# The first normalisation and the first convolution columns run quarter by quarter of the features while their modulation weights load

## The chip, the cores and the metric

The kernel runs on one core of one Trainium2 chip. The metric is the device time in microseconds (us) of one launch, the median of several runs. PE is TensorE, with its weight loads listed apart as PEld; DVE is VectorE, ACT is ScalarE, POOL is GpSimd and SP is SyncE. "Clock" is the TensorE clock that was granted, as a share of 2.4 GHz: 0.50 is 1.2 GHz.

## The reference

Two sets of 128 tokens with 2048 features each, context tokens and latent tokens, go through two layers of a diffusion backbone. A conditioning vector makes six modulation vectors for each layer.

```
mod = silu(c) @ w_ada[l] + b_ada[l]          # 2048 x 12288: shift1, scale1, gate1, shift2, scale2, gate2
h   = rms_norm(x, g_attn) * (1 + scale1) + shift1
u_conv, q_g, k_g, v_g, q_w, k_w, v_w = split(h @ w_in[l])   # 2048 x 3584; the first 1024 columns are u_conv
a, gt = split(u_conv);  y = depthwise_conv31(a * sigmoid(gt)) ; layer norm; silu
... two attentions, both with grouped heads ...
x = x + gate1 * (concat(y_conv, y_g, y_w) @ w_out[l])
x = x + gate2 * (relu(h2 @ w_mlp1)**2 @ w_mlp2)     # h2: second modulated norm
```

After the two layers comes a last rms_norm. Everything is float32.

## The kernel before

**Tiles and products.** Features lie on partitions: `xT[128, 16, 256]` holds feature tile k for the 256 tokens. A large product splits both factors into a rounded part (`hi`, `hs[..., 0:256]`) and a rest (`lo`, `hs[..., 256:512]`) and sums three products: hi by both parts in one matmul of 512 columns, lo by the rounded part in one of 256. A weight matrix is used in pairs of 2 x 256 columns. Each pair is 8 slices of 512 rows by 256 columns: slice o is loaded by SP into `raw` (four slots of two slices, 1 MiB each, gated on `lo_ready`), copied by ACT into `hi` (`split_hi`, gated on `half_used` of three slices earlier), subtracted by DVE into `lo` (`split_lo`), and used by PE. The slots `hi` and `lo` hold four slices. The column pairs of `w_in` are seven, so its products have 56 steps of one slice. The first two pairs are the convolution's a and gate columns.

**Modulation vectors.** One vector is 16 units of `w_ada` of 128 rows by 2048 columns, 1 MiB each. The product of a unit is four matmuls, on four strips of 32 output partitions (`ada_products`). When the 16 units of a vector are summed, ACT copies the bank to `rows`, PE turns it (`ada_turn`) and DVE adds the bias (`add_bias`, counted in `mods_done`). Vectors 0 and 1 (shift1 and scale1) are loaded before anything else by POOL into eight slots (`pre_a`, `pre_q`, `ada`; `PRE_SLOTS`). A unit's slot is refilled when PE has used the unit eight before (`ada_used`). Later vectors use the two slots of `ada`, and their units are put behind certain steps of the products: `units_behind(step)` gives two units behind steps 2, 6, 10 and so on and a single one behind steps 36, 44, 48 and 52, 32 units in all.

**Order at the start.** PE: vector 0's units, transposes of the small parameters (`vrows`), `ada_turn(0)`, transposes of x, vector 1's units, `ada_turn(1)`, the sums of squares over features (`norm_sums`), `spread_rstd`, then step 0 of `w_in`. DVE makes the sums of squares in one reduction of `xsq`, and after vector 1 the normalised tiles of `hs`, 16 tiles one after another with ACT (`norm`). SP issues the small parameters, then x, and it holds the first `w_in` slots back with one wait:

```
sp.wait_ge(ada_used, 4 * PRE_JOBS - PRE_SLOTS - 1)     # 23 units used
```

**The 56 steps of `w_in` in one layer.** Each engine walks the same steps in `mixers(l)`, each followed by `mix_ops(l, step)`. DVE: step 9 and 17 `gate` (a times sigmoid of the gate columns, from `zc` in SBUF), then the 30 remaining taps of the convolution for two channel pairs, by `TAP_PLAN`: two taps of the first pair in steps 10 to 17, one in 18 to 31; one of the second pair in steps 18 to 45 (two in 33 and 34). A tap is two instructions of 128x256. From step 20 on come the squares, roots, rotations and scores of the heads. ACT copies half of each bank to `tmp` and DVE adds the other half, every four steps. The third vector's `ada_rows`, `ada_turn` and `add_bias` stand at steps 31, 32 and 33. The cached keys are turned at step 10.

Of the kernel before, what the change touches and what calls it, by code (L numbers as in the profile page):

```python
# [21 lines left out]
f32 = mybir.dt.float32  # L22
# [5 lines left out]
P = 128  # L28
S = 2
# [35 lines left out]
SINGLE_UNITS = (9, 11, 12, 13)  # L65

SHIFT1, SCALE1, GATE1, SHIFT2, SCALE2, GATE2 = (KT * n for n in range(6))

C_ID, C_PERM, C_COS, C_SIN, C_SEL = 0, 128, 256, 384, 512
CONSTS = 520  # L70
# [29 lines left out]
def build(nc, t):  # L100
# [45 lines left out]
    eps = place("eps", [P, 1], f32)  # L146
    warm = place("warm", [P, 1], f32)
    eps_sum = place("eps_sum", [P, 1], f32)
# [9 lines left out]
    xtok = place("xtok", [P, S, D], f32, hs_at)  # L158

# [21 lines left out]
    xsq = place("xsq", [P, KT, TOK], f32, hs_at + 16384)  # L181
# [5 lines left out]
    rstd_cols = pb[7][:, TOK:TOK + P], pb[6][:, 0:P]  # L187

# [4 lines left out]
    sel = cst[:, C_SEL:C_SEL + 8]  # L193

# [26 lines left out]
    x_turned, x_ready, xsq_ready, ssq_set = sem("x_turned"), sem("x_ready"), sem("xsq_ready"), sem("ssq_set")  # L221
# [45 lines left out]
    def units_behind(step):  # L267
# [9 lines left out]
        return []  # L277

# [20 lines left out]
    def vectors_done(layer, vector):  # L299

        return layer * VECTORS + vector // KT + 1
# [21 lines left out]
    def sums_left_out(layer, kind):  # L323


        return 2 * (2 * layer + (kind in ("up", "down")))
# [12 lines left out]
    with block:  # L339
# [3 lines left out]
        def _(sp):  # L343
            sp.dma_start(craw[:, 0, :], t["c_ctx"].rearrange("(p t) -> p t", t=KT)).then_inc(c_in, 16)
            sp.dma_start(craw[:, 1, :], t["c"].rearrange("a (p t) -> (a p) t", t=KT)).then_inc(c_in, 16)
            sp.dma_start(cst[:, :], t["consts"]).then_inc(consts_in, 16)
            sp.dma_start(sinks[:, :, :].rearrange("p l h -> p (l h)"),
# [15 lines left out]
            for s, name in enumerate(("x_prompt", "x_sample")):  # L363
                sp.dma_start(xtok[:, s, :], t[name].rearrange("a q d -> (a q) d")).then_inc(x_in, 16)
            sp.wait_ge(ada_used, 4 * PRE_JOBS - PRE_SLOTS - 1)

            for l in range(DEPTH):
# [5 lines left out]
                def load_mixers(l):  # L373
                    n = l * PAIRS_LAYER
                    for p in range(IN):
# [32 lines left out]
        def _(pool):  # L408
# [6 lines left out]
            src = t["w_ada"][0].rearrange("(p k) n -> p k n", k=KT)  # L415
            for u in range(4 * PRE_JOBS):
                after(pool, ada_used, u - PRE_SLOTS + 1)
                pool.dma_start(pre[u % PRE_SLOTS], src[:, u % KT, u // KT * D:(u // KT + 1) * D])\
                    .then_inc(pre_landed[u % PRE_SLOTS], 16)
# [7 lines left out]
        def _(pe):  # L427
            def norm_sums(l, c):


                final = (l, c) != (0, -2)
                if final:
                    pe.wait_ge(ssq_steps, ssq_base(l, c) + 1 + KT - 2)
                else:
                    pe.wait_ge(ssq_set, 1)
                for s in range(S):
                    mm = pe.matmul(pb[7][:, s:s + 1], ssq[:, s * P:(s + 1) * P], ones[:, 0:1],
                                   start=True, stop=not final)
                    for j in range(2 * final):
# [6 lines left out]
            def spread_rstd(q):  # L446
                pe.wait_ge(tok_rstd_ready, q + 1)
                for s in range(S):
                    pe.matmul(rstd_cols[s], tok_rstd[:, s:s + 1].to_broadcast([P, P]), ident,
                              start=True, stop=True).then_inc(rstd_spread, 1)  # L450
# [6 lines left out]
            def ada_unit(l, m, a, k):  # L457

                if k == 0:
                    pe.wait_ge(mods_done, l * VECTORS + m)  # L460
# [9 lines left out]
            def pre_vector(m):  # L470


                after(pe, mods_done, m)
                for k in range(KT):
                    u = KT * m + k
                    pe.wait_ge(pre_landed[u % PRE_SLOTS], 16 * (u // PRE_SLOTS) + 16)
                    ada_products(k, pre[u % PRE_SLOTS])

            def ada_turn(v):

                pe.wait_ge(rows_ready, v + 1)
# [8 lines left out]
            pre_vector(0)  # L490
            pe.wait_ge(vecs_in, 16 * 10 * DEPTH)
            for l in range(DEPTH):
                for b, r in ((0, P), (1, P), (2, MISC)):
                    mm = pe.transpose(pb[5 + 2 * l][:, b * P:b * P + r], vrows[0:r, l, b, :], ident[0:r, 0:r])
                mm.then_inc(vecs_turned, 1)
            ada_turn(0)
# [8 lines left out]
            pre_vector(1)  # L505
            ada_turn(1)

            for l in range(DEPTH):
# [63 lines left out]
                def mixers(l):  # L572
                    n = l * PAIRS_LAYER
                    for step in range(8 * IN):
                        p, g, h = step // 8, step // 4 % 2, step % 4
                        if h == 0:
# [7 lines left out]
                        for u in units_behind(step):  # L584
# [33 lines left out]
                def mix_ops(l, step):  # L618
# [3 lines left out]
                    if step == 10:  # L622
# [20 lines left out]
                    if step == 32:  # L643
# [106 lines left out]
                def stage(name, c, l=l):  # L750
                    if name in ("norm1", "norm2"):
                        norm_sums(*((l, -1) if name == "norm2" else (l - 1, CHUNKS - 1) if l else (0, -2)))
# [14 lines left out]
        def _(act):  # L767
            def split_hi(n, o):

                s, sub = chunk_place(n, o)  # L770
                act.wait_ge(raw_landed[s], 16 * (n + o // 8 + 1))
# [3 lines left out]
            def ada_rows(v):  # L775
                act.wait_ge(ada_used, KT * v + KT)
                after(act, modps_ready, v)
# [4 lines left out]
            ada_rows(0)  # L782
# [5 lines left out]
            for b in range(8):  # L788
                s, q = b % 2, b // 2
                act.wait_ge(x_turned, b + 1)  # L790
                act.activation(xT[:, 4 * q:4 * q + 4, s * P:(s + 1) * P],
                               pb[b % 4][:, :].rearrange("p (k q) -> p k q", k=4), ACT.Copy).then_inc(x_ready, 1)
            act.wait_ge(x_ready, 8)
            act.activation(xsq[:, :, :], xT[:, :, :], ACT.Square).then_inc(xsq_ready, 1)
            ada_rows(1)
            for o in range(3):
                act.wait_ge(raw_landed[o // 2], 16)
                act.activation(hi[:, o, :, :], raw[:, o // 2, 4 * (o % 2):4 * (o % 2) + 4, :], ACT.Copy)\
                   .then_inc(hi_ready, 1)

            for l in range(DEPTH):
# [63 lines left out]
                def mix_ops(l, step):  # L865
# [3 lines left out]
                    if step == 0:  # L869
# [4 lines left out]
                    if step in (8, 16):  # L874
# [3 lines left out]
                    if step == 11:  # L878
                        drain_turn(1, kcT[:, :, :], "p (v d) -> p v d", v=4)
                    if step == 20:  # L880
                        act.wait_ge(bank_freed, n4 + 10)
                        act.wait_ge(conv_tap, TAP_OPS * l + TAPS_DONE[17])
# [13 lines left out]
                    if step == 31:  # L896
# [107 lines left out]
                def norm(q, shift, l=l):  # L1004
                    act.wait_ge(stat_ready, q + 1)
# [3 lines left out]
                    for k in range(KT):  # L1009
                        for s in range(S):  # L1010
                            act.wait_ge(norm_y, q * NORM_STEPS + S * k + s + 1)
                            act.activation(hs[:, k, s * P:(s + 1) * P], ybuf[:, 2 * (k % UNROLL_K) + s, :], ACT.Identity,
                                           bias=mods[:, l, shift + k, s:s + 1]).then_inc(norm_hi, 1)

                def stage(name, c, l=l):
                    if name == "norm1":
# [6 lines left out]
            act.wait_ge(stat_ready, 2 * DEPTH + 1)  # L1023
# [12 lines left out]
        def _(dve):  # L1036
# [7 lines left out]
            def add_bias(l, m):  # L1044

                dve.wait_ge(modps_ready, l * VECTORS + m + 1)
# [14 lines left out]
            for s in range(S):  # L1061
                dve.tensor_tensor(cT[:, :, s:s + 1], craw[:, s, :].unsqueeze(2), csig[:, s, :].unsqueeze(2),
                                  ALU.mult).then_inc(c_ready, 1)
            dve.wait_ge(sinks_in, 16)
            own.done(dve.tensor_scalar(nsinks[:, :, :], sinks[:, :, :], -1.0, None, ALU.mult))
            dve.wait_ge(vecs_ready, 1)
            add_bias(0, 0)
            dve.wait_ge(xsq_ready, 1)
# [396 lines left out]
```

## Time and profile before

| | us |
|---|---|
| median of the runs (3 runs, 2327.01 to 2327.36) | 2327.07 |
| the profiled execution's own time | 2326.37 |
| its span, first to last instruction | 2324.7 |
| PE busy | 2254.8 (97%) |
| DVE busy | 1459.3 (63%) |
| ACT busy | 1096.3 (47%) |

The profiled execution is 0.7 us below the median, and 1.7 us of its time lie outside its span. All stretches below are in us from the start of the span. The opening is the stretch up to 122 us; steps 3 to 55 of the first layer's `w_in` follow it.

### The profile page before, as it was taken

How to read it: one execution, taken by the hardware profiler on the slowest of the kernel's cores; microseconds unless marked ns; L12 is line 12 of the kernel's file. 1: busy time of each engine (PE TensorE's matmuls, PEld its weight loads, DVE VectorE, ACT ScalarE, POOL GpSimd, SP SyncE). 2: the span in 40 equal slices, each digit the busy share in tenths (PEclk: the TensorE clock that was granted, in tenths of full speed). 3: DMA queues.
4: the chain of work that ended last, by engine and by line, in shares of the span. 5: the costliest groups of instructions: out<-in, count | busy, mean ns of one | idle time of the engine just before them, and what ended most of it. 6: DMA issues, size and time to landing. Idle time of an engine off the chain costs nothing.

```text
span 2324.7 us, 36272 instructions
## 1 busy us (share of the span) xinstructions
PE 2254.8 (97%) x13442; PEld 1831.4 (79%) x13442; DVE 1459.3 (63%) x2521; ACT 1096.3 (47%) x1739; POOL 101.9 (4%) x196
## 2 busy tenths in 40 slices
PE   5799999999999999999999999999999999999998
PEld 0378777778887887887787777887788888888887
DVE  0379655655655665565567876667566666666665
ACT  0344564544444444444445445645445444445444
POOL 2000000000000000000000000000000000000000
PEclk7699999999999999999999999999999999999999
DMA  9988868698589679768955877566956556655652
GB/s 384 366 317 290 292 232 323 230 334 283 192 278 316 209 223 327 250 193 299 315 182 194 328 286 264 197 197 228 317 175 186 183 184 201 192 181 185 195 188 102
DMA packets 390005, 570.66 MB, mean 245 GB/s; under 512 B 9540, under 2 KB 364408, under 8 KB 365048
## 3 DMA queue, kind: packets, MB, share of 16 engines
q1 hardware_dynamic: 359928, 365.51, 49.0%
q0 software_dynamic: 27648, 201.34, 21.9%
q10 hardware_dynamic: 2304, 2.10, 0.3%
q8 instruction: 85, 1.39, 0.2%
q14 instruction: 40, 0.33, 0.0%
HBM read 565.76 MB, written 3.15 MB: 245 GB/s over the span
## 4 chain that ended last, share of the span: by engine, by line
PE 90%; DVE 4%; DMA 4%; ACT 2%; issue 1%; POOL 0%; ACTq 0%; POOLq 0%
PE bank L530 44%; PE bank L533 21%; PE bank L607 9%; PE bank L466 6%; PE bank L610 4%; DMA ada<-in_w_ada 4%; DVE hs L1321 1%; DVE ybuf L1313 1%; PE bank L551 1%; PE bank L554 1%; ACT hi L773 0%; DVE lo L1041 0%; PE bank L730 0%; PE bank L483 0%; PE bank L707 0%
## 5 line engine op out<-in xcount | busy, mean ns | idle before, releaser
L1041 DVE TENSOR_TENSOR lo<-raw,hi 128x1024 fp32r<-128x1024 f32 x685 | 820.8, 1223 | 400.7 <-ACT hi L773 400.3
L773 ACT ACTIVATE hi<-raw 128x1024 fp32r<-128x1024 f32 x685 | 706.3, 1054 | 447.3 <-PE bank L533 314.8
L530 PE MATMUL bank<-act,hi 128*128 128x512 f32 x2304 | 724.7, 396 | 1.2 <-DVE tsum L1160 1.2
L530 PE MATMUL bank<-hs,hi 128*128 128x512 f32 x2048 | 652.2, 400 | 7.8 <-DVE hs L1321 4.5
L533 PEld LDWEIGHTS bank<-act,lo 128*128 128x128 f32 x2304 | 432.8, 188 | 102.4
L533 PEld LDWEIGHTS bank<-hs,lo 128*128 128x128 f32 x2048 | 386.7, 189 | 92.3
L533 PE MATMUL bank<-act,lo 128*128 128x256 f32 x2304 | 452.7, 278 | 0.0
L533 PE MATMUL bank<-hs,lo 128*128 128x256 f32 x2048 | 404.3, 279 | 0.0
L530 PEld LDWEIGHTS bank<-act,hi 128*128 128x128 f32 x2304 | 350.7, 189 | 5.6 <-issue 4.2
L530 PEld LDWEIGHTS bank<-hs,hi 128*128 128x128 f32 x2048 | 313.4, 190 | 43.7 <-issue 37.2
L607 PE MATMUL bank<-hs,hi 128*128 128x512 f32 x896 | 292.9, 408 | 7.9 <-DVE hs L1321 4.6
L826 ACT ACTIVATE tmp<-bank 128x256 f32<-128x256 f32 x336 | 110.7, 382 | 395.9 <-PE bank L533 318.1
L1095 DVE TENSOR_TENSOR tsum<-bank,tmp 128x256 f32<-128x256 f32 x272 | 114.5, 421 | 207.6 <-ACT tmp L826 207.6
L610 PEld LDWEIGHTS bank<-hs,lo 128*128 128x128 f32 x896 | 170.3, 190 | 40.6
L610 PE MATMUL bank<-hs,lo 128*128 128x256 f32 x896 | 178.1, 280 | 0.0
L466 PE MATMUL bank<-ada,cT 128*32 128x512 f32 x1344 | 168.4, 615 | 8.6 <-DMA ada<-in_w_ada 8.6
L607 PEld LDWEIGHTS bank<-hs,hi 128*128 128x128 f32 x896 | 139.3, 191 | 23.0 <-issue 13.7
L413 POOL DMA_DIRECT2D ada<-in_w_ada x160 | 84.7, 529 | 1510.2 <-PE bank L466 1482.7
L832 ACT ACTIVATE thid<-xT 128x256 f32 (+1 forms) x160 | 66.9, 418 | 163.0 <-DVE xT L1127 153.4
L1127 DVE SCALAR_TENSOR_TENSOR xT<-tsum,mods,xT 128x128 f32 (+1 forms) x304 | 93.5, 349 | 36.2 <-DVE tsum L1095 34.9
L1238 DVE SCALAR_TENSOR_TENSOR yconv<-hpad,vecs,yconv 128x256 f32<-128x256 f32 x240 | 100.9, 477 | 0.0
L466 PEld LDWEIGHTS bank<-ada,cT 128*32 128x32 f32 x1344 | 34.3, 110 | 76.4 <-issue 42.9
(151 smaller groups left out, 1174.1 us busy)
## 6 DMA issues: line engine op xcount, KB each, us to landing
raw<-in_w_mlp SPq DMA_DIRECT2D x256, 1024.0 KB, 5.9
ada<-in_w_ada POOLq DMA_DIRECT2D x168, 1024.0 KB, 7.6
raw<-in_w_in SPq DMA_DIRECT2D x56, 1024.0 KB, 5.3
raw<-in_w_out SPq DMA_DIRECT2D x32, 1024.0 KB, 5.6
pre_a<-in_w_ada POOLq DMA_DIRECT2D x16, 1024.0 KB, 17.0
pre_q<-in_w_ada POOLq DMA_DIRECT2D x8, 1024.0 KB, 17.8
xtok<-in_x_prompt SPq DMA_DIRECT2D x1, 1024.0 KB, 14.2
xtok<-in_x_sample SPq DMA_DIRECT2D x1, 1024.0 KB, 32.5
```

The lines of the kernel that those rows point to most:

```text
L413: pool.dma_start(ada[:, k % 2, :], src[:, k, bass.ds(m * D, D)]).then_inc(ada_landed[k % 2], 16)
L466: mm = pe.matmul(ada_ps[32 * q:32 * q + 32, :], cT[:, k, :], unit[:, q * 512:(q + 1) * 512], start=(k == 0), stop=(k == KT - 1))
L530: pe.matmul(pb[2 * g + j][:, :], hi[:, h, k, j * P:(j + 1) * P], acts[:, k_, :], start=(k_ == 0), stop=False)
L533: mm = pe.matmul(pb[2 * g + j][:, TOK:2 * TOK], lo[:, h, k, j * P:(j + 1) * P], acts[:, k_, 0:TOK], start=False, stop=(k_ == KT - 1))
L607: pe.matmul(pb[2 * g + j][:, :], hi[:, slot, k, j * P:(j + 1) * P], acts[:, 4 * x + k, :], start=start, stop=False)
L610: mm = pe.matmul(pb[2 * g + j][:, TOK:2 * TOK], lo[:, slot, k, j * P:(j + 1) * P], acts[:, 4 * x + k, 0:TOK], start=False, stop=stop)
L773: act.activation(hi[:, o % 4, :, :], raw[:, s, 4 * sub:4 * sub + 4, :], ACT.Copy).then_inc(hi_ready, 1)
L826: act.activation(tmp[:, j, :], pb[2 * g + j][:, TOK:2 * TOK], ACT.Copy).then_inc(tmp_ready, 1)
L1041: dve.tensor_tensor(lo[:, o % 4, :, :], raw[:, s, 4 * sub:4 * sub + 4, :], hi[:, o % 4, :, :].bitcast(f32), ALU.subtract).then_inc(lo_read ...
L1095: dve.tensor_tensor(tsum[:, j, :], bank, tmp[:, j, :], ALU.add).then_inc(bank_freed, 1)
L1127: dve.scalar_tensor_tensor(x, total[:, :, s * P:(s + 1) * P], mods[:, l, bass.ds(gate + 4 * i + 2 * g + j, 1), s], x, ALU.mult, ALU.add).t ...
L1238: dve.scalar_tensor_tensor(y, hpad[:, ch, :, tap:tap + P], vecs[:, l, 1, 4 * tap + ch:4 * tap + ch + 1], y, ALU.mult, ALU.add).then_inc(co ...
```

## The change

- A unit of the first two vectors is now a quarter q of both: 2 x 128 rows by 512 columns of vector 0 and 512 columns of vector 1, in two transfers of POOL. Eight units make one quarter. There are still 32 units, 1 MiB each, in eight slots.
- x is loaded ahead of the small parameters on SP's queue and turned first on PE. DVE, no longer ACT, copies its banks. ACT squares `xtok` with a running sum over features (`accum_out`), so PE's `norm_sums` and DVE's reduction fall away for the first norm.
- When quarter q is summed, its four feature tiles of shift1 and scale1 are made (`quarter_turn`, one `rows` copy, a bias add), DVE and ACT normalise tiles 4q to 4q+3, and PE runs four slices on them (`open_chunk`): the same four k tiles for all four column groups of the two convolution pairs. The four groups stay open in banks 0 to 3 over all quarters. Between the slices stand the next quarter's units.
- An open slice adds both halves of `hs` into one 256-column range: six matmuls of 256 columns for each k and j pair, not two of 512 and two of 256. No `tmp` copy and no add follow. ACT takes the sigmoid and DVE the product `a * sigmoid(gt)` straight from PSUM (`open_gate`).
- SP loads the 16 open slices in 8 slots, each in two transfers, gated one by one on `ada_used` (`RAW_GATES`).
- Steps 0 to 15 of the first layer no longer exist in `mixers`. Two units of vector 2 stand behind slice 13, the other 30 behind steps 18 to 54 (`UNITS_FIRST`: alternately 2 and 1 on even steps). The first layer's taps are one of each pair in every step 16 to 45. The rows, turn and bias add of vector 2 stand at steps 35, 35 and 36; the cached keys are turned at step 18.

```diff
+RAW_GATES = (5, 6, 12, 14, 20, 22, 28, 30)
 @@ sync
+            for s, name in enumerate(("x_prompt", "x_sample")):      # now ahead of sinks and vrows
+                sp.dma_start(xtok[:, s, :], ...).then_inc(x_in, 16)
-            sp.wait_ge(ada_used, 4 * PRE_JOBS - PRE_SLOTS - 1)
+            for j in range(OPEN_STEPS // 2):
+                after(sp, lo_ready, 2 * j - 6)
+                sp.wait_ge(ada_used, RAW_GATES[j])
+                for g in range(2):
+                    sp.dma_start(raw[:, j % 4, 4 * g:4 * g + 4, :], w_conv[:, j // 2, g, :, j % 2, :])...
 @@ gpsimd
-                pool.dma_start(pre[u % PRE_SLOTS], src[:, u % KT, u // KT * D:(u // KT + 1) * D])...
+                for m in range(2):
+                    pool.dma_start(unit[:, :, m, :], src[:, 2 * kk:2 * kk + 2, m, 512 * q:512 * q + 512])...
 @@ tensor
+            for u in range(8):
+                quarter_unit(u)
+            pe.wait_ge(vecs_ready, DEPTH)
+            spread_rstd(0)
+            quarter_turn(0)
+            for q in range(QUARTERS - 1):
+                for o in range(4 * q, 4 * q + 3):
+                    open_chunk(o)
+                    for u in (0, 1) if o % 4 < 2 else (0, 1, 2, 3):
+                        quarter_unit(8 * (q + 1) + 2 * (o % 4) + u)
+                quarter_turn(q + 1)
+                open_chunk(4 * q + 3)
+            for o in range(12, 16):
+                open_chunk(o)
+                if o == 13:
+                    for u in range(OPEN_UNITS):
+                        ada_unit(0, 2, PRE_JOBS, u)
 @@ scalar
+            for q in range(QUARTERS):
+                act.wait_ge(ada_used, 8 * q + 8)
+                after(act, modps_ready, q)
+                act.activation(rows[:, :], ada_ps[:, :], ACT.Copy).then_inc(rows_ready, 1)
+                act.wait_ge(mods_done, q + 1)
+                norm_tiles(0, SHIFT1, 0, range(4 * q, 4 * q + 4))
+                for o in range(4 * q + (2 if q else 0), 4 * q + 6):
+                    split_hi(0, o, o < OPEN_STEPS)
+                    if o == 16:
+                        open_sigmoid(0)
+            split_hi(0, 18)
+            open_sigmoid(2)
 @@ vector: the same loop with the bias add, gains(), norm_tiles(), split_lo() and open_gate()
-                    for step in range(8 * (IN + 1)):
+                    for step in range(OPEN_STEPS if l == 0 else 0, 8 * (IN + 1)):
```

## Rows read from the trace of the kernel before

**Rows 1.** Busy time by stretch: start:end, length, engines, granted clock, DMA share, GB/s

```profile
22.00:54.00 32.00, 19.08 (x88) 2.04 (x88) 0.00 (x0) 0.00 (x0) 5.28 (x10) 0.55 1.01 418
64.00:68.00 4.00, 4.00 (x42) 1.24 (x44) 0.00 (x0) 3.97 (x3) 1.58 (x3) 1.00 1.01 426
75.00:97.00 22.00, 14.31 (x64) 1.57 (x64) 0.82 (x1) 0.03 (x1) 0.86 (x2) 0.58 1.03 414
107.00:110.00 3.00, 3.00 (x10) 2.52 (x10) 3.00 (x13) 1.95 (x7) 0.00 (x0) 0.50 0.82 290
...
165.20:222.10 56.90, 56.90 (x353) 44.73 (x352) 51.47 (x101) 24.99 (x34) 4.22 (x8) 1.00 0.81 294
222.10:281.80 59.70, 59.70 (x395) 47.82 (x393) 41.90 (x91) 31.79 (x66) 4.22 (x8) 1.00 0.81 299
```

**Rows 2.** The chain that ended last, from 74 us to step 3

```profile
74.81 20.11 DMA ada<-in_w_ada
...
94.97 1.98 PE bank L466 x8
96.97 0.61 ACT rows L778
...
97.62 1.89 PE bank L483 x8
...
119.55 1.57 DVE hs L1321 x6
```

**Rows 3.** DMA in 0:95, then 24:70, 75:90 and 95:98: packets, MB, share

```profile
DMA packets 7779, 37.86 MB, mean 399 GB/s; under 512 B 1172, under 2 KB 3297, under 8 KB 3425
q0 software_dynamic: 4608, 33.56, 85.7%
...
DMA packets 2919, 19.42 MB, mean 422 GB/s; under 512 B 356, under 2 KB 562, under 8 KB 562
...
q0 software_dynamic: 764, 5.55, 87.6%
q1 hardware_dynamic: 763, 0.78, 14.6%
...
DMA packets 1151, 1.16 MB, mean 387 GB/s; under 512 B 16, under 2 KB 1151, under 8 KB 1151
```

**Rows 4.** The timeline: start, length, engine, line, instructions merged

```profile
9.10 7.96 SPq L362 DMA_DIRECT2D vrows<-in_conv_b  x1
...
26.98 0.53 POOL L418 DMA_DIRECT2D ada<-in_w_ada  x1 [2.31 <-PE bank L466]
...
104.19 1.81 DVE L1313 SCALAR_TENSOR_TENSOR ybuf<-xT,amul,bank 128x128 f32<-128x128 f32 x6 [0.89 <-PE bank L449]
...
106.68 1.19 PE L607 MATMUL bank<-hs,hi 128*128 128x512 f32 x2 [2.09 <-DVE hs L1321]
...
108.09 1.05 PE L607 MATMUL bank<-hs,hi 128*128 128x512 f32 x2
...
109.38 1.05 PE L607 MATMUL bank<-hs,hi 128*128 128x512 f32 x2
...
148.73 0.66 PE L691 MATMUL bank<-cst,ktokc 128*128 128x128 f32 x4
...
160.46 1.92 PE L466 MATMUL bank<-ada,cT 128*32 128x512 f32 x16
...
165.20 0.63 PE L607 MATMUL bank<-hs,hi 128*128 128x512 f32 x2
...
167.99 0.63 PE L607 MATMUL bank<-hs,hi 128*128 128x512 f32 x2
...
430.97 0.64 PE L551 MATMUL bank<-act,hi 128*128 128x256 f32 x4
...
431.69 0.64 PE L551 MATMUL bank<-act,hi 128*128 128x256 f32 x4
```

**Rows 5.** DVE and ACT in the steps of `w_in`

```profile
147.04 1.06 ACT L773 ACTIVATE hi<-raw 128x1024 fp32r<-128x1024 f32 x1 [1.72 <-PE bank L610]
...
159.29 1.21 DVE L1041 TENSOR_TENSOR lo<-raw,hi 128x1024 fp32r<-128x1024 f32 x1
160.43 1.66 DVE L1238 SCALAR_TENSOR_TENSOR yconv<-hpad,vecs,yconv 128x256 f32<-128x256 f32 x4
```

**Rows 6.** Issue to landing of `ada`, us min/median/max, 120 to 330 us

```profile
DMA to landing us min/median/max: 4.9/6.8/10.5
```

More of the change, by code:

```diff
@@ L265, in mixer_vector, with units_behind @@
         return layer * VECTORS + (2 if layer == 0 else 3)
-    def units_behind(step):
+    def units_behind(l, step):
+        if l == 0:
+            return [FIRST_UNIT[step] + u for u in range(UNITS_FIRST.get(step, 0))]
         half = step // 4
@@ L299, in vectors_done @@
     def vectors_done(layer, vector):
-        return layer * VECTORS + vector // KT + 1
+        return event(layer * VECTORS + vector // KT + 1)
     def q_rstd(h):
@@ L1008, in norm @@
                     act.wait_ge(mods_done, vectors_done(l, shift))
[L1009 to L1013, printed above, removed]
+                    norm_tiles(q, shift, l, range(KT))
                 def stage(name, c, l=l):
-                    if name == "norm1":
+                    if name == "norm1" and l:
                         norm(2 * l, SHIFT1)
@@ new lines, in first_tap, with clear_halo @@
+            def first_tap(l, first):
+                for ch in (first, first + 1):
+                    dve.tensor_scalar(yconv[:, ch, :].rearrange("p (s q) -> p s q", s=S),
+                                      hpad[:, ch, :, 0:P], vecs[:, l, 1, ch:ch + 1],
+                                      vecs[:, l, 1, V_CONVB + ch:V_CONVB + ch + 1], ALU.mult, ALU.add)\
+                       .then_inc(conv_tap, 1)
+            def clear_halo():
+                own.done(dve.memset(hpad[:, :, :, 0:HALO].rearrange("p c s q -> p (c s) q"), 0.0))
+                own.done(dve.memset(hpad[:, :, :, HALO + P:2 * HALO + P].rearrange("p c s q -> p (c s) q"), 0.0))
@@ new lines, in gate @@
+            def gate(l, first, a):
+                own.wait(own.n)
+                dve.wait_ge(gate_sig, 2 * l + first // 2 + 1)
+                dve.tensor_tensor(
+                    hpad[:, first:first + 2, :, HALO:HALO + P].rearrange("p c s q -> p (c s) q"), a,
+                    zc[:, CT + first:CT + first + 2, :].rearrange("p c (s q) -> p (c s) q", s=S), ALU.mult)\
+                   .then_inc(conv_gated, 1)
+                dve.wait_ge(conv_gated, 2 * l + first // 2 + 1)
+                first_tap(l, first)
@@ L1139, in mixers @@
                     n = l * PAIRS_LAYER
-                    for step in range(8 * (IN + 1)):
+                    for step in range(OPEN_STEPS if l == 0 else 0, 8 * (IN + 1)):
                         p, g = step // 8, step // 4 % 2
@@ L1395, in tap_plan @@
                     count[tap, ch] = n
-        done[step] = n
     assert n == TAP_OPS and next(a, None) is None and next(b, None) is None
-    return plan, count, done
+    return plan, count
 HEAD_GROUPS = (0, 1, 2, 3, 4, 5, 6, 8, 10)
-TAP_PLAN, TAP_COUNT, TAPS_DONE = tap_plan()
+TAP_PLAN, TAP_COUNT = zip(*(tap_plan(layer) for layer in range(DEPTH)))
 ROPES = ((26, KG), (28, QG), (30, QG + 2), (34, QG + 4), (42, KW), (46, WIN_Q[0]), (49, WIN_Q[2]), (53, WIN_Q[4]))
```

331 lines of the change are left out of this document (195 added, 136 removed).

## The prediction, made before the changed kernel was run

> **What bounds the kernel now.** I read the page first: PE is busy 97% of the span, so the whole is bound by TensorE, and the only stretch where a change can win much is one in which PE has no work or works slowly. The busy time by stretch finds it. From 22 to 54 us PE is busy 19.1 of 32 us at a granted clock of 0.55, from 75 to 97 us 14.3 of 22 us at 0.58, and in both the DMA share is 1.0 at 418 and 414 GB/s [rows 1]. The reader is to see there that the opening is bound by the transfer of `w_ada`, and that PE's low figure is a queue that waits for it. The chain that ended last says the same: it runs through a landing of `ada` for 20.1 us up to the last unit at 94.97, then through `rows`, the turn, and DVE's 16 tiles up to 121 us [rows 2]. After that nothing but PE counts: from 165.2 to 281.8 us it is busy for all 116.6 us at full clock [rows 1].
>
> So the opening costs 122 us in which PE does three slices of `w_in` and the vectors' products. The change puts 16 slices in there. PE work that it takes out of the time behind is worth its full length; what it adds to the transfer costs its full length as well, since DMA is the bound.
>
> **Reference point.** Step 16 starts at 165.20 and step 17 at 167.99, so a slice is 2.79 us at full clock [rows 4]. I work out when step 16 starts in the new kernel.
>
> **The transfer of the opening.** By 95 us 37.86 MB have moved, of which 33.56 MB are the 32 units [rows 3]; x (2.10 MB) and the small parameters (about 0.4 MB) are in the rest, which leaves 1.8 MB of `raw`. In the new order the last unit is preceded by seven of the eight open `raw` slots (7.34 MB), since the eighth is gated on 30 used units. That is 33.56 + 2.1 + 0.4 + 7.34 = 43.4 MB, 5.5 MB more, and at 415 GB/s 13.4 us. The runs of a unit shrink from 8 KB to 2 KB. No row shows 2 KB: 8 KB runs went at 422 GB/s and 1 KB runs alone at 387 [rows 3]. The ends are 0 and 7.2 us for 33.56 MB; I take 410, nearer to the large runs since a queue of many runs kept its rate at 1 KB within 8%, so 2.3 us. The last unit then lands at 94.9 + 13.4 + 2.3 = 110.6 us. Each unit is also two transfers now. The trace shows 32 units in 95 us, 2.9 us each with eight outstanding, so no fixed time for each transfer is visible when others are queued behind it, and I add none.
>
> The Trainium skill, "DMA: Bandwidth & Descriptors", section "Anatomy of one DMA", gives a fixed 2.0 us for each transfer plus its bytes at 436 GB/s and, in "Bandwidth", advises at least 1 MiB for each transfer, which speaks against cutting the units in two. Taken one after another, 64 transfers would be an estimated 205 us, and already the 32 of before would be 141 us, where the trace has 95; so the trace disagrees for a full queue, and the sum goes by the trace.
>
> **What may keep the queue from being full.** (a) The start. x lies ahead of the small parameters now. Before, q0's and q1's packets alternated one for one from 75 to 90 us (764 and 763) although one was eight times as long [rows 3], so with 2 KB units x's long runs get the larger share, and the SP stall of 7.96 us at a small parameter [rows 4], which I read as its short runs waiting one by one behind 8 KB runs, should shrink. I place x at 10 to 14 us and the first unit's use at 22 to 28 us, before the eight slots are full at about (8.4 + 2.5) / 0.42 + 3 = 29 us. No bubble. If x landed only at 30 us, PE would start at 39 and DMA would idle 10 us; this end stays in the range. (b) PE's order. ACT splits slices 4 and 5 before it copies `rows` of quarter 1. Their slot is gated on 12 used units, needs some 7 us to land (the median of `ada` under such load is 6.8 [rows 6]) and 2.1 us to split [rows 5], while PE needs about 6.6 us (a slice and four units). PE stands for a few us, and the same again in quarters 2 and 3. The eight slots ahead hold 20 us of transfer, which covers most of it. I add 2.5 us (0 to 8). Last unit landed: 113.1.
>
> (c) POOL issues 512 runs for a unit instead of 128. A unit's issue took 0.53 us [rows 4]; the ends are 1.1 us (by transfer) and 2.1 us (by run), both under the 2.5 us that a unit's bytes take. Nothing.
>
> **PE in the opening.** One quarter at full clock: four slices at 0.72 us for each k (430.97 to 431.69, the same six-matmul form), 2.88 each and 11.5 together; eight units at 0.93 (1.85 for two), 7.4; turn and wait for `rows` 1.6. Sum 20.5 us. At 1.2 GHz a k takes 1.29 (108.09 to 109.38), a unit 1.98 and the turn 1.89: 38 us [rows 2, 4]. DMA needs (8.39 + 2.1) / 0.415 = 25.3 us for a quarter. Warm, PE is hidden with 5 us to spare; cold, it is the bound. With 20.5 of 25.3 us busy, in dense pieces, I expect mostly full clock: the dense stretch from 64 to 68 us had 1.00, the ones with 60% and 65% busy 0.55 and 0.58 [rows 1].
>
> The Trainium skill, "TensorE: Matmul & The Clock Gate", Part 1, says that the array starts throttled and that sustained activity releases it; the rows at 64 and at 75 us agree in direction. It would leave the sum as it is.
>
> DVE in a quarter: 4.2 us of tiles (1.04 each) and four `lo` of 1.21, 9 of 25 us; ACT less. Both are hidden, as are the x copies, the squares and the removed reduction.
>
> **Behind the last unit.** 113.1 + product 1.98 + `rows` 0.61 + turn 1.89 (half clock, since PE waited for transfers [rows 2]) = 117.6. Slice 11 at the half clock's 1.29 for each k: 5.1, to 122.7. DVE's first tile is ready 0.4 + 2.5 us after the turn (104.19 to 106.68 [rows 4]), 120.5, so slice 11 covers it. Slices 12 to 15: 11.5, and two units 1.85. Step 16 starts at 136.1 instead of 165.2: 29.1 us earlier.
>
> **What is owed later.** Before step 16 the old kernel had done eight units of vector 2, the new one two: 6 x 0.93 = 5.6 us. The turn of the cached keys moves behind: 0.6 us. The first layer's other 40 steps are the same products. The bias add of vector 2 now stands at DVE's step 36, and PE's unit behind step 36 waits for it: behind the start of step 36 come `hi` 1.06, `lo` 1.21, four taps 1.66 and the add 0.19, 4.1 us [rows 5], against 2.8 us of products. 1.5 us (0 to 3).
>
> **Steps 16 to 45.** DVE had 93.4 us of work in 116.6 us [rows 1]; 24 more tap instructions at 0.42 minus a gate of 1.4 make 102, and PE gets five more units, 121. Not the bound in the sum; within a step it is 1.21 + 1.66 against 2.79 and more. DMA: 30 slices (15 MiB) and 21 units are 37.7 MB in 121 us, 312 GB/s, below 415. Nothing.
>
> **Sum.** 29.1 - 5.6 - 0.6 - 1.5 = 21.4 us. Against the profiled execution: 2326.4 - 21.4 = 2305.0; its median stood 0.7 us higher, so 2305.7 us.
>
> **Rivals.**
> 1. *All orders hidden, PE warm to the end.* No 2.5 us, no 1.5 us, slice 11, the turn and the unit at full clock (2.2 + 0.9 + 1.0): 29.5 us gained, 2297.6. For it speaks the backlog of eight slots; against it that PE waits for single units at the end, as from 75 to 97 us.
> 2. *PE becomes the bound of the opening by its clock.* If half of a quarter's work runs at 1.2 GHz, it takes 29.3 us, 4.0 more than DMA, three times: 12 us, 2318. Waits for `raw` between slices would keep it so. At 1.2 GHz throughout, 12.7 x 3 = 38 us are lost: 2344, slower than before. It ends slower from 68% of the work at 1.2 GHz on.
> 3. *A unit's two transfers of 2 KB runs take longer than its bytes*, in POOL's issue or in the queue. From 4.2 us for a unit on (134.5 / 32) the change loses; at 5 us the last unit lands at 160: 2353. Rows for 1 KB runs at 387 GB/s and 0.53 us of issue speak against it.
> 4. *Later steps wait.* `ada` has two slots; a unit needs 6.8 us from issue (median), and behind steps 18 to 36 the next one is due after two slices and a unit, 5.6 to 6.6 us. Up to 1.2 us at nine places is 11 us: 2317. Before, the same density stood only in steps 44 to 54, which are longer.
> 5. *The gain is eaten whole*, by 10 us of idle transfer at the start and rival 2 in part: 2326.
>
> **How the numbers follow.** Forecast 0.42, with a range of its own from 2300 to 2311; rival 1 0.17; rival 2 0.15 in part and 0.03 as slower; rival 3 0.04; rival 4 0.15; rival 5 0.04. A change of 0.2% (4.7 us) is about what the measurement tells from none. Slower is rival 2's end, rival 3 and a share of 5: 0.08; same 0.05, faster 0.87. The range reaches from a little below rival 1 (2294, with 422 GB/s kept) to just past 2 and 4 (2320), and leaves out 3, 5 and 2's end.
>
> **What would show it.** The last product of a quarter unit should start near 113 us and step 16 near 136; DMA share 1.0 from 3 to 110 us, at 410 GB/s or more; clock above 0.8 from 45 to 100 us; PE busy all the way from step 16 with a gap of 1 to 3 us at step 36 only. A last unit past 125 us shows rival 2, 3 or the bubble: by the clock, by POOL's instructions, or by a DMA share below 1 near 30 us. Waits of PE for `ada` behind steps 20 to 36 show rival 4.

## The result and the profile after

| | before | after |
|---|---|---|
| median of the runs, us | 2327.04 (4 runs, 2326.48 to 2327.36) | 2344.68 (4 runs, 2343.03 to 2346.91) |
| the profiled execution and its span, us | 2326.37, 2324.7 | 2343.03, 2341.3 |
| last unit of vectors 0 and 1 used, us | 96.9 | 151.8 |
| step 16 starts, us | 165.2 | 170.8 |
| second norm of layer 0 (`spread_rstd`), us | 447.2 | 463.4 |

The ratio is 1.0077, 95% interval 1.0059 to 1.0094: slower by 17.6 us, where 21.4 us less was forecast. By the two profiled executions step 16 comes 5.6 us later, and from there to the second norm it takes 292.6 us instead of 282.0, 10.6 more. What follows adds 0.4. That makes the 16.6 us between the spans.

Busy time by stretch of the changed kernel, with the columns of [rows 1]:

```profile
3.00:151.00 148.00, 82.16 (x582) 57.12 (x586) 33.54 (x78) 28.56 (x49) 44.58 (x62) 0.78 0.78 295
...
30.00:40.00 10.00, 6.90 (x38) 2.29 (x42) 0.00 (x0) 0.81 (x2) 2.66 (x4) 0.58 0.30 106
50.00:60.00 10.00, 0.00 (x0) 0.00 (x0) 0.93 (x2) 1.78 (x2) 0.00 (x0) 0.50 1.04 411
66.00:70.00 4.00, 4.00 (x35) 2.56 (x35) 2.36 (x2) 2.00 (x2) 2.66 (x4) 1.00 0.27 81
80.00:90.00 10.00, 0.00 (x0) 0.00 (x0) 0.00 (x0) 0.00 (x0) 2.92 (x5) 0.64 1.04 410
96.00:100.00 4.00, 4.00 (x21) 4.00 (x21) 4.00 (x14) 3.02 (x8) 0.00 (x0) 0.51 0.09 30
100.00:110.00 10.00, 10.00 (x83) 6.86 (x83) 1.69 (x2) 1.06 (x1) 3.78 (x6) 1.00 0.44 128
120.00:130.00 10.00, 0.67 (x4) 0.67 (x4) 2.12 (x2) 2.49 (x3) 0.22 (x1) 0.52 1.04 411
140.00:150.00 10.00, 10.00 (x88) 6.94 (x88) 0.00 (x0) 0.00 (x0) 0.00 (x0) 1.00 0.32 105
...
170.77:463.40 292.63, 288.18 (x1858) 223.98 (x1856) 196.69 (x382) 142.67 (x253) 24.32 (x46) 1.00 0.85 306
```

Before, the transfer was full throughout the opening and PE filled in behind it. Here the two take turns. From 50 to 60, from 80 to 90 and nearly all of 120 to 130 us PE does nothing while the transfer is full. From 66 to 70, from 100 to 110 and from 140 to 150 PE is busy all the time at full clock while the transfer runs at 0.27, 0.44 and 0.32. Over 148 us it moves 295 GB/s, 43.7 MB: the amount that was forecast (43.4), not the rate (410 and more).

The chain of waits says what PE stands for (start, length, what):

```profile
18.80 14.25 DMA vrows<-in_g_final
...
41.62 16.58 DMA raw<-in_w_in
...
73.25 16.94 DMA raw<-in_w_in
...
91.17 1.04 ACT hi L843
...
92.75 1.87 PE bank L512 x8
...
110.15 16.62 DMA raw<-in_w_in
...
148.20 2.76 PE bank L503 x24
```

Where [rows 2] had landings of `ada`, here stand three landings of an open slot of `raw`, each some 16.7 us (from the issue of its second half), and one of the small parameters. PE's waits from 10 to 350 us (what, total us, times, longest):

```profile
PE bank L512 <- ACT rows L880: 27.3, 3, 13.3
PE bank L527 <- DVE lo L1126: 15.1, 1, 15.1
PE bank L556 <- DMA vrows<-in_g_final: 13.7, 1, 13.7
PE bank L550 <- DMA xtok<-in_x_sample: 13.5, 1, 13.5
PE bank L491 <- DMA ada<-in_w_ada: 1.6, 3, 0.9
PE bank L491 <- DVE mods L1133: 1.0, 1, 1.0
```

The first line is the one to read with care. PE waits for ACT's copy of `rows`, which takes 0.6 us; ACT stands before it at `split_hi` of slices 4q+4 and 4q+5, and those wait for `raw`. The timeline has the step:

```profile
90.21 2.00 ACT L843 ACTIVATE hi<-raw 128x1024 fp32r<-128x1024 f32 x2 [21.82 <-DMA raw<-in_w_in]
92.12 0.58 ACT L880 ACTIVATE rows<-bank 128x512 f32<-128x512 f32 x1
```

And the packets, from 73.2 to 90.2 us, while the chain waits for its second slot; q0 is POOL's queue of units, q1 is SP's queue of `raw`:

```profile
DMA packets 2846, 6.80 MB, mean 400 GB/s; under 512 B 198, under 2 KB 1521, under 8 KB 2845
...
q0 software_dynamic: 1490, 5.42, 80.4%
q1 hardware_dynamic: 1355, 1.35, 22.9%
```

As in [rows 3] the two queues get about one packet each in turn. A packet of q0 is now 3.6 KB (5.42 MB / 1490), one of q1 is 1 KB, so `raw` gets a fifth of the bytes, 79 GB/s. Within one burst of work PE has released the units' slots, and POOL has filled its queue with the next units. The Trainium skill, "DMA: Bandwidth & Descriptors", section "Queues, rings and completion order", says that a DMA engine goes round its queues packet by packet; the counts agree. A `raw` slot is 1024 packets, and by equal counts they come with 1024 packets of units: 1024 x 4.6 KB at 400 GB/s is an estimated 12 us. The page has 16.6 as the median of the 16 transfers, two for each slot:

```profile
raw<-in_w_in SPq DMA_DIRECT2D x16, 512.0 KB, 16.6
```

The packets say where the rest goes. The slot's first half is issued at 72.84, and up to 75.0 us q1 moves nothing. By 86.4 it has moved 1015 packets, so the slot's 1024 are through near 86.5:

```profile
q1 hardware_dynamic: 1015, 1.02, 22.2%
```

It counts as landed only at 90.2 us, when some 300 packets more than its own (1355 less 1024) have moved on q1, for the next slot. So of the 17.4 us from the first issue some 3 pass ahead of the first packet, 11 in the sharing and 3.7 behind. The other two slots have about 3, 12 and 2. Why a slot starts 3 us after its issue and counts as landed so late isn't shown.

Then comes the other half of the turn-taking. By 96 us the units have landed as well, and POOL's next issue is at 104.18, since PE first does the turn and two slices and frees no slot before that:

```profile
104.18 2.88 POOL L447 DMA_DIRECT2D pre_a<-in_w_ada  x4 [21.26 <-PE bank L503]
```

### The profile page after: what moved, and what is told of

It reads as the page before. It is cut to its first block, busy times and chain, and to the rows that moved or that the text cites. A ratio compares the mean times of both kernels' runs of the same rounds, so it can differ in the third digit from the quotient of the medians.

```text
span 2341.3 us, 36628 instructions
## 1 busy us (share of the span) xinstructions
PE 2242.5 (96%) x13582; PEld 1844.6 (79%) x13582; DVE 1455.8 (62%) x2525; ACT 1090.4 (47%) x1728; POOL 131.0 (6%) x228
## 4 chain that ended last, share of the span: by engine, by line
PE 88%; DMA 4%; DVE 4%; ACT 2%; SPq 1%; issue 1%; ACTq 0%; POOLq 0%; POOL 0%; DVEq 0%
PE bank L598 43%; PE bank L601 21%; PE bank L677 7%; PE bank L491 6%; PE bank L680 3%; DMA raw<-in_w_in 2%; DMA ada<-in_w_ada 2%; PE bank L619 1%; PE bank L527 1%; DVE hs L1182 1%; DVE ybuf L1174 1%; PE bank L503 1%; ACT hi L843 1%; PE bank L622 1%; DMA vrows<-in_g_final 1%
## 5 line engine op out<-in xcount | busy, mean ns | idle before, releaser
L598 PE MATMUL bank<-hs,hi 128*128 128x512 f32 x2048 | 652.4, 400 | 7.7 <-DVE hs L1182 4.4
L601 PEld LDWEIGHTS bank<-hs,lo 128*128 128x128 f32 x2048 | 386.8, 189 | 92.3
L601 PE MATMUL bank<-hs,lo 128*128 128x256 f32 x2048 | 404.4, 279 | 0.0
L598 PEld LDWEIGHTS bank<-hs,hi 128*128 128x128 f32 x2048 | 313.6, 190 | 43.5 <-issue 36.8
L677 PE MATMUL bank<-hs,hi 128*128 128x512 f32 x768 | 250.7, 408 | 3.7 <-DVE hs L1182 2.1
L680 PEld LDWEIGHTS bank<-hs,lo 128*128 128x128 f32 x768 | 145.4, 189 | 34.4
L491 PE MATMUL bank<-ada,cT 128*32 128x512 f32 x1280 | 155.9, 599 | 2.8 <-DMA ada<-in_w_ada 1.8
L680 PE MATMUL bank<-hs,lo 128*128 128x256 f32 x768 | 152.3, 280 | 0.0
L677 PEld LDWEIGHTS bank<-hs,hi 128*128 128x128 f32 x768 | 119.4, 191 | 17.3 <-issue 12.3
L907 ACT ACTIVATE act<-thid 128x256 fp32r<-128x256 f32 x128 | 53.5, 418 | 67.2 <-DVE thid L1254 67.2
## 6 DMA issues: line engine op xcount, KB each, us to landing
raw<-in_w_in SPq DMA_DIRECT2D x16, 512.0 KB, 16.6
```

The lines of the kernel that those rows point to most:

```text
L491: mm = pe.matmul(ada_ps[32 * q:32 * q + 32, :], cT[:, k, :], unit[:, q * 512:(q + 1) * 512], start=(k == 0), stop=(k == KT - 1))
L598: pe.matmul(pb[2 * g + j][:, :], hi[:, h, k, j * P:(j + 1) * P], acts[:, k_, :], start=(k_ == 0), stop=False)
L601: mm = pe.matmul(pb[2 * g + j][:, TOK:2 * TOK], lo[:, h, k, j * P:(j + 1) * P], acts[:, k_, 0:TOK], start=False, stop=(k_ == KT - 1))
L677: pe.matmul(pb[2 * g + j][:, :], hi[:, slot, k, j * P:(j + 1) * P], acts[:, 4 * x + k, :], start=start, stop=False)
L680: mm = pe.matmul(pb[2 * g + j][:, TOK:2 * TOK], lo[:, slot, k, j * P:(j + 1) * P], acts[:, 4 * x + k, 0:TOK], start=False, stop=stop)
```

## The experiments

Each was compared with the kernel before on its own chip (medians there 2327.48, 2327.52 and 2327.74 us). The ratio is to the kernel before; that of the changed kernel is 1.0077. "Step 16" is its start in the profiled execution.

| | median (range, runs) | ratio, 95% | step 16 |
|---|---|---|---|
| e1 | 2313.47 (2311.17 to 2317.93, 4) | 0.9944, 0.9928 to 0.9961 | 139.6 |
| e2 | 2331.48 (2328.11 to 2334.60, 10) | 1.0015, 1.0005 to 1.0024 | 157.3 |
| e3 | 2337.22 (2335.45 to 2339.12, 4) | 1.0046, 1.0029 to 1.0063 | 162.7 |
| e4 | 2331.76 (2330.62 to 2334.05, 10) | 1.0020, 1.0010 to 1.0030 | not the same opening |
| e5 | 2331.71 (2330.51 to 2336.64, 9) | 1.0019, 1.0009 to 1.0029 | 158.5 |
| e6 | 2308.23 (2306.92 to 2308.31, 4) | 0.9917, 0.9901 to 0.9934 | 135.3 |
| e7 | 2314.18 (2309.76 to 2319.23, 4) | 0.9950, 0.9933 to 0.9967 | 136.3 |
| e8 | 2315.14 (2313.64 to 2316.70, 4) | 0.9949, 0.9933 to 0.9966 | 134.0 |
| e9 | 2313.05 (2308.53 to 2313.52, 5) | 0.9932, 0.9919 to 0.9946 | 139.2 |

**e1: the open `raw` slots are issued early.** The first four slots are issued with no gate, the others eight used units sooner, and the gate of 30 used units stands behind them.

```diff
-RAW_GATES = (5, 6, 12, 14, 20, 22, 28, 30)
+RAW_GATES = (0, 0, 0, 0, 12, 14, 20, 22)
-                sp.wait_ge(ada_used, RAW_GATES[j])
+                after(sp, ada_used, RAW_GATES[j])
+            sp.wait_ge(ada_used, 30)
```

> The changed kernel, but each open raw slot is asked for about eight used units earlier: the first four as soon as SP is through the small parameters, the others at 12, 14, 20 and 22 used units; the pairs behind still wait for 30. Theory A (the slots are asked for too late; a slot takes 16.6 us to land beside POOL's backlog, PE stands for it three times, 42 us in all, and the transfers then stand for want of free units): the three waits go, the last unit is used near 118 us instead of 151, step 16 starts near 140 instead of 171, and the time is 2307 to 2318 us. Theory B (the waits come from the order of ACT's and DVE's work; the landing is not what is late): the waits stay within a few us, 2335 to 2345. Theory C (the transfers as such are slower in the new form): DMA share 1.0 throughout but the last unit past 135 us.

31.2 us less than the changed kernel in the median, and step 16 31.2 us earlier. PE's waits and the busy time by stretch:

```profile
PE bank L528 <- DVE lo L1127: 6.0, 1, 6.0
...
PE bank L513 <- ACT rows L881: 2.2, 3, 0.7
```

```profile
3.00:116.00 113.00, 75.75 (x578) 49.92 (x578) 35.69 (x80) 29.81 (x50) 45.14 (x63) 0.91 1.03 403
```

The wait for `rows` falls from 27.3 to 2.2 us, which is three copies; the one for `lo` from 15.1 to 6.0. The transfer is full to the last unit. A slot still takes 15.1 us to land, median of the page: the landing hasn't become shorter, it lies where nobody waits for it. The mean clock in the opening rises from 0.78 to 0.91 with no edit to PE, so the low clock was a sequel of the waits. The result is theory A's.

**e2: the small parameters are turned after the first quarter's units.** Only PE's order is changed.

```diff
+            for u in range(8):
+                quarter_unit(u)
             pe.wait_ge(vecs_in, 16 * 10 * DEPTH)
             ... transposes of vrows ...
-            for u in range(8):
-                quarter_unit(u)
```

> The changed kernel, but PE uses the first eight units before it waits for the small parameters and turns them. PE stood 14 us for them, and the transfers stood from about 31 to 37 us. Theory A (idle transfer in the opening is lost for good): the first unit is used near 20 us, as soon as it has landed and the turns of x are done, the transfers do not stop near 30 us, and 5 to 10 us are gained: 2335 to 2340 us. Rival (the slots of raw set the pace, so what is gained at the start is lost again in the first wait for raw): within 2 us of 2344.7.

13.2 us less than the changed kernel: the wait for `vrows` was worth its length. The first unit is used at 18.9 us instead of 34.8, and the wait for `rows` stays at 26.9 us. It is more than either theory had (5 to 10 us, or within 2).

**e3: each quarter splits its own slices only.** ACT and DVE copy `rows` and add the bias of the next quarter before they split that quarter's slices.

```diff
-                for o in range(4 * q + (2 if q else 0), 4 * q + 6):
+                for o in range(4 * q, 4 * q + (6 if q == 3 else 4)):
```

> The changed kernel, but ACT and DVE split slices 4q and 4q+1 in their own quarter, behind its normalised tiles, so that the copy of rows for the next quarter no longer stands behind slices whose raw slot is late. Theory A (the landing itself is late): the waits move from the turn to the first slice of each quarter, PE gets one slice and a turn ahead but pays for the split behind the tiles; 2338 to 2345 us. Theory B (the order was the fault): the waits of 13 us at the turns vanish and are not found elsewhere; 2315 to 2325.

7.5 us less. The wait changes its name and mostly stays:

```profile
PE bank L527 <- DVE lo L1126: 33.7, 4, 15.2
...
PE bank L512 <- ACT rows L880: 2.2, 3, 0.7
```

The three landings on the chain are 16.6, 16.0 and 16.6 us. The waits at `rows` and `lo` are 35.9 us instead of 42.4. So ACT's order costs some 7 us of them, and the rest is the landing, which is only seen at another place. Theory A's mechanism holds, with a little more gained than it had.

**e4: the kernel before, each of its 32 units cut into two transfers of 2 KB runs** (abridged).

```diff
-                pool.dma_start(pre[u % PRE_SLOTS], src[:, u % KT, ...])...
+                for m in range(2):
+                    pool.dma_start(unit "p (b m n)"[:, :, m, :], src "p (b m n)"[:, :, m, :])...
```

> The kernel before, but every one of its first 32 units is loaded in two transfers of 512 KB with runs of 2 KB, to the same places. Measures the disputed price of the new form of the transfers by itself. Theory A: 2 to 7 us of lower rate (410 to 390 GB/s instead of 422 over 33.6 MB), the opening's last unit at 97 to 102 us instead of 95: 2329 to 2334 us. Theory C (a fixed 2 us for each transfer, or a slow issue by POOL): 20 us and more, 2347 us or above. With no price at all: 2327.

4.3 us more than the kernel before in the median, and the last unit's product starts at 100.03 instead of 94.97 us. Packets from 0 to 100 us, and by queue from 70 to 100:

```profile
DMA packets 13583, 39.08 MB, mean 391 GB/s; under 512 B 1701, under 2 KB 5004, under 8 KB 13324
...
q0 software_dynamic: 2599, 9.44, 77.2%
q1 hardware_dynamic: 2772, 2.80, 26.3%
```

By 100 us 39.08 MB have moved, 1.2 MB more than by 95 us before [rows 3], and q0's part of both is the 32 units' 33.56 MB. The 1.2 MB are `raw`, which got ahead by one packet for each, now smaller, packet of a unit: 3 of the 5 us. The other 2 are the rate, 391 GB/s against 399. Thirty-two more transfers for 4.3 us are 0.13 us each. The rule of the Trainium skill that the prediction weighed, a fixed 2.0 us for each transfer ("DMA: Bandwidth & Descriptors", section "Anatomy of one DMA"), would have had 64 us for them; it doesn't show while others are queued.

**e5: half of each open slot is issued on ACT's queue.** The gates are those of the changed kernel.

```diff
-                for g in range(2):
-                    sp.dma_start(raw[:, j % 4, 4 * g:4 * g + 4, :], ...)
+                sp.dma_start(raw[:, j % 4, 0:4, :], ...)            # SP: first half
+            def open_half(j):                                       # ACT: second half
+                act.wait_ge(ada_used, RAW_GATES[j])
+                act.dma_start(raw[:, j % 4, 4:8, :], ...)
```

> The changed kernel, but the second half of each open raw slot is issued by ACT on its own queue, under the same gates; SP issues the first half. In the changed kernel the queue of raw got one packet for each of POOL's (705 and 709 from 82 to 90 us), 1 KB against 3.6 KB, so a slot landed 16.6 us after its issue. Theory A1 (the share of the queue sets the landing): two queues get two packets for one of POOL's, a slot lands in 8 to 10 us, the three waits of PE shrink by 6 to 8 us each, and the time is 2320 to 2330 us. Theory A2 (a slot lands only when the units queued ahead of it are through): the landing stays at 15 to 17 us, and the time within 3 us of 2344.7.

13.0 us less than the changed kernel. From 40 to 56 us three queues share, and the chain has shorter landings:

```profile
q0 software_dynamic: 1290, 4.68, 77.3%
q1 hardware_dynamic: 720, 0.72, 12.8%
q10 hardware_dynamic: 714, 0.71, 12.7%
```

```profile
41.57 12.79 DMA raw<-in_w_in
...
68.12 12.89 DMA raw<-in_w_in
...
100.51 12.53 DMA raw<-in_w_in
```

With the same bytes, gates and backlog a slot lands 3.8 to 4.1 us sooner, three times, and PE's waits for `rows` and for the first slice fall from 42.4 to 29.5 us. Equal counts on three queues would have 512 packets of each beside the slot's halves, 512 x 5.6 KB at 400 GB/s, an estimated 7 us instead of 12. So a second queue takes off about a quarter of the landing, nearly what the counts give. That is less than theory A1 had (8 to 10 us for a landing, 2320 to 2330), since by the packets of the changed kernel some 5 us of a landing lie ahead of and behind the sharing; A2 is out.

**e6: e1 and e2 together.**

> Both edits at once: the raw slots asked for early, and the first eight units used before the small parameters. Theory (the transfer is now the only bound of the opening; the early run's DMA share is already 1.0 from 20 to 120 us): the earlier start of PE brings nothing more or 1 to 3 us, last unit used at 112 to 116 us, 2309 to 2314 us. Rival (the 14 us wait of PE at the start is on the path): another 8 to 13 us, 2300 to 2305.

36.5 us less than the changed kernel, 19.3 less than the kernel before: the fastest of all. It is less than the sum of e1 and e2, 44.4 us, and lies between the theory (2309 to 2314) and the rival (2300 to 2305): the transfer is now full from 3 to 113 us, and from 100 to 116 us PE is busy without a gap too, so little is left to gain from either alone:

```profile
3.00:113.00 110.00, 79.90 (x558) 54.55 (x559) 33.53 (x78) 27.57 (x48) 44.70 (x62) 0.84 1.03 403
100.00:116.00 16.00, 16.00 (x136) 10.63 (x137) 4.73 (x7) 4.01 (x4) 0.00 (x0) 1.00 0.90 349
```

```profile
114.71 1.90 PE L504 MATMUL bank<-ada,cT 128*32 128x512 f32 x16
117.33 1.06 PE L513 MATMUL bank<-cst,rows 128*128 128x4 f32 x8 [0.72 <-ACT rows L881]
```

The last turn ends at 118.4 us, where the prediction's sum had 117.6, and step 16 starts at 135.3, where it had 136.1.

**e7: e6, e3's order, and the last two slots late** (gates 22 and 28), to keep the bytes of the last slices behind the last units.

> As the run with both edits, and ACT and DVE split slices 4q and 4q+1 in their own quarter, with the last two open slots gated at 22 and 28 used units. Theory (bytes ahead of the last unit set its landing; with the split in its own quarter a late slot no longer blocks the rows): up to 1 MiB less ahead of the last unit, 2 us earlier, but 2 to 3 us more behind the last quarter's tiles: 2309 to 2315 us, the same as without.

Not faster than e6, and within the forecast. The wait for `rows` falls to 2.1 us, and the one for `lo` rises to 14.8 us at four places; step 16 is 1.0 us later. In the median it is 5.9 us slower than e6, with a wide range (2309.76 to 2319.23); its profile, at the lower end of it, shows 2.5 us by the second norm.

**e8: e6 with one unit of vector 2 behind each of the steps 18 to 31 and 34 to 49**, its `rows` and turn at step 32 and its bias add at 33.

```diff
-UNITS_FIRST = {18: 2, 20: 1, 22: 2, 24: 1, 26: 2, ...}
-VECTOR_STEP = (34, 31)
+UNITS_FIRST = {step: 1 for step in (*range(18, 32), *range(34, 50))}
+VECTOR_STEP = (31, 31)
```

> As the run with both edits, but the 30 later units stand one behind each of steps 18 to 31 and 34 to 49, and vector 2's rows, turn and bias at steps 32, 32 and 33. In the changed kernel PE waited 1 us for the bias add at step 36 and 2 to 4 us for landings of ada. Theory (pairs of units in two slots leave 6.6 us for a landing of 7.2): the bias wait goes and the ada waits mostly: 2 to 4 us less than the run with both edits. Rival (these waits cost nothing at the end, since the heads' steps behind are set by other work): within 1 us of it.

6.9 us slower than e6, all of it behind step 16: 299.7 us to the second norm against 292.1. PE waits for `ada` at five places and for ACT's `esink`, a wait of 0.4 us in the changed kernel:

```profile
PE bank L491 <- DMA ada<-in_w_ada: 3.3, 5, 1.0
...
PE bank L788 <- ACT esink L1080: 3.1, 3, 1.4
```

The wait for the bias add is gone, but what took its place costs more: 3.7 us of idle time and 3.9 of busy time over e6. A unit that stands alone takes PE 1.06 us, two together 1.85 (e6); the 46 units up to the second norm take 47.4 us here and 45.3 in the changed kernel. Neither the theory (2 to 4 us less) nor the rival (within 1 us) held: even spacing is not what the later steps lack.

**e9: e6 with slices 0 and 1 split ahead of the first `rows`**, and gates (0, 0, 0, 0, 8, 8, 16, 16).

> As the run with both edits (raw slots early, small parameters late; 2308.2 us), and slices 0 and 1 are split ahead of the first rows copy and the first bias add, and the later four open slots are asked for at 8, 8, 16 and 16 used units instead of 12, 14, 20 and 22. In the run with both edits PE still stood 6.0 us for the first slice's lo and 6.3 us for rows behind late slots, and from 100 to 120 us it was busy without a gap while the DMA share fell to 0.79, so PE sets the end of the opening there. Theory (these two waits are what is left before PE): 5 to 8 us less PE time ahead of the last unit, which the transfer (43.4 MB at 0.41 MB/us, 109 us) allows to about 110 instead of 115.7: 2302 to 2305 us. Rival (the transfer already sets it): within 1.5 us of 2308.2.

Not faster than e6: 4.8 us slower in the median, but the fastest of its runs, 2308.53, is near e6's, and the two intervals of the ratio overlap. Both the theory (2302 to 2305) and the rival (within 1.5 us of e6) miss. In the profiled one step 16 is 3.9 us later. ACT, and with it the first `rows`, now waits for a slot (6.4 us of the 8.6 that PE waits for `rows`). More `raw` ahead of the last units may also put these back; that is not shown by itself. The chain, with the turn at half clock again:

```profile
95.28 20.59 DMA ada<-in_w_ada
...
118.56 1.87 PE bank L513 x8
```

## Why the prediction was wrong

**The step that failed** is (b) of "what may keep the queue from being full", PE's order. It saw the mechanism: `rows` of the next quarter stands behind the split of slices 4 and 5, whose slot is issued with some 6.6 us of PE work left. It then put the slot's landing at "some 7 us", from the median of `ada` [rows 6], and let "the eight slots ahead" cover most of the rest: 2.5 us in all (0 to 8). Both parts were wrong. The landing is 16.6 us and more. [Rows 6] are from the steps of `w_in`, where two units are outstanding; in the opening POOL has up to eight queued, and the prediction itself had the row for that, a landing of `ada` of 20.11 us on the chain [rows 2]. The kernel before even has the same stream in the same place: its first two slots of `raw`, issued from 71.4 us on beside the last units, land after 24.8 us in the median:

```profile
raw<-in_w_in SPq DMA_DIRECT2D x2, 1024.0 KB, 24.8
```

And the backlog that was to cover the wait is what makes the slot slow: PE works off eight units in one go, POOL queues eight new ones, the `raw` slot issued in the middle has to share with them. When PE goes on they have landed or nearly so, and PE has a turn and slices to do before it frees their slots again. In this time the transfer has little or nothing: 0.27 from 66 to 70, 0.09 from 96 to 100, 0.44 and 0.32 in the windows. The waits are 27.3 us at `rows` and 15.1 us at the first slice, 42.4 in all; e1, which only issues these slots sooner, gives back 31.2.

**The start, (a).** x landed as placed (PE waits for it 13.5 us), the queue was not: the small parameters held PE until 33.1 us, and the first unit was used at 34.8, outside the "22 to 28". The prediction took the 7.96 us stall at a small parameter as the thing that shrinks (it is 5.71 us now) and did not add up their landing, 14.25 us on the chain, behind which PE's program puts the first unit. The transfer was empty for some 7 of the 10 us from 30 to 40, near the end that the range named for a late x ("DMA would idle 10 us"), and the first part of rival 5. e2 prices it at 13.2 us with the `raw` gates in place, since these gates count used units and move with it, and e6 against e1 at 5.2 us without.

**Rival 2** was right in what it named ("waits for `raw` between slices would keep it so") and wrong in its price, which was a clock's. Its slower end, 2344, is the measured time to 1 us, but that is chance: it took all PE work at 1.2 GHz, while the trace has 0.78 on average: the turn at 92.75, right behind a wait, takes the 1.87 us of half clock, but the dense stretches from 100 to 110 and from 140 to 150 have 1.00.

**Rival 3** had its mechanism in part. The 2 KB runs cost 4.3 us by e4, not 2.3, within the ends of 0 and 7.2. POOL takes 1.44 us for a unit, inside the 1.1 to 2.1, and no PE wait shows for it:

```profile
37.08 1.44 POOL L447 DMA_DIRECT2D pre_a<-in_w_ada  x2 [24.05 <-PE bank L503]
```

What the cut units cost in the changed kernel beyond this, as packets half as long that `raw` meets one for one, is to the good of `raw`: beside packets of 7.3 KB a queue of 1 KB ones had an eighth of the bytes [rows 3], not a fifth.

**Owed later.** 10.6 us instead of 7.7. It is about the same in all kernels with the change and its spacing of units (292.1 to 292.9 us from step 16 to the second norm in e1, e2, e3, e6 and e9, 293.1 in e5, 293.6 in e7), so it hardly depends on the opening. In the trace PE is busy 7.5 us more there than before, and idle 3.1 us more:

```profile
165.20:447.20 282.00, 280.68 (x1806) 222.54 (x1804) 187.91 (x359) 142.35 (x254) 21.26 (x40) 1.00 0.81 290
```

Of the busy time the units of vectors take 6.4 us, where the forecast had 5.6 for six:

```profile
L466 PE MATMUL bank<-ada,cT 128*32 128x512 f32 x320 | 38.9, 599 | 0.0
L491 PE MATMUL bank<-ada,cT 128*32 128x512 f32 x368 | 45.3, 600 | 2.5 <-DMA ada<-in_w_ada 1.6 <-DVE mods L1133 1.0
```

More of them stand alone now, at 1.06 us each (eight single ones in `UNITS_FIRST`, four before), which would go with it. The keys' turn takes 0.7, and 0.4 stay unexplained. Of the idle time 1.0 us is the bias add at step 36 (forecast 1.5), 1.6 are waits for `ada` at three places, the rest single waits of 0.4 us and less. The waits for `ada` are rival 4, with 1.6 us instead of up to 11: a unit lands in 6.7 us there, about as in [rows 6].

**What held.** The gain of the idea, with the slots and the small parameters out of its way, is e6's: 29.9 us at step 16 where 29.1 were forecast, 10.1 owed where 7.7 were, 19.5 of span in all where 21.4 were; the median moved by 19.3. The last unit's product starts in e6 near 115.7, forecast 113.1. The transfer's size (43.4 MB) and its rate with a full queue (403 GB/s, a little under the 410 taken) were right. Slices 12 to 15 take 0.72 for each k, as placed. The turn and slice 11 ran at the full clock and not at half, as rival 1 had them (the turn 1.05 us in the changed kernel and 1.06 in e6, forecast 1.89), since PE did not wait for the last units.

**What stays open.** Why a slot of `raw` moves its first packet some 3 us after its issue and counts as landed 2 to 4 us after its last; and whether some other spacing than e8's wins back the 2.6 us of idle there.

## What to carry to other kernels

Take the landing time of a transfer from a stretch with the same backlog: a transfer of 1 MiB of `raw` lands in 5.3 us (median) in the later steps of the changed kernel, and one of 512 KB in 16.6 us beside POOL's full queue. Where a small stream is gated on the progress of a large one, issue it before the large one's queue fills, as early as its buffers allow (e1); a gate that is to keep it from taking bandwidth can cost its whole landing once the consumer has to stand for it. And a wait named after a short instruction (`rows`, 0.6 us) is to be followed to what that engine stood for before it.

## What the runs showed of the hardware

- Queues with work share by packets, not by bytes. Beside each other, POOL's queue and SP's had 1490 and 1355 packets, 5.42 and 1.35 MB. A second queue for the small stream brought it 1434 packets against 1290, and landings of 12.5 to 12.9 us for 16.6 to 16.9.
- Runs of 2 KB don't make 2 KB packets on POOL's queue: 3.6 KB is the mean. In e4 the 33.56 MB of the units are 9216 packets, which is what 8192 of two runs (4 KB) and 16 small ones for each of the 64 transfers add up to; in [rows 3] 4608 packets, by the same count 4096 of 8 KB and 512.
- A transfer of POOL with 256 runs of 2 KB takes 0.72 us to issue, one with 128 runs of 8 KB 0.53 [rows 4].
- In the changed kernel the granted clock is 0.50 in the wait from 50 to 60 us and 1.00 in the dense work from 100 to 110. Here it is a result of the order of the waits: e1, which only issues `raw` earlier, raised the opening's mean from 0.78 to 0.91. In e6, where PE starts earlier and waits for single units, the mean is 0.84.
